# Attention output formed transposed, and the SSD half of the output projection done early

## What is computed

```
hn = rms_norm(x, norm_mix);  q, k, v, z, xbc, dt = split(hn @ w_in)
attn = rms_norm(softmax(q k^T / 8) v, attn_norm)            # 8 heads of 64, 2 kv heads; norm over 512
y = ssd_fwd + ssd_bwd + xs * d_skip                          # 8 heads of 64, chunks of 128
ssm = rms_norm(y * silu(z), ssm_norm)                        # in two groups of 256
x1 = x + concat(attn, ssm) @ w_out
h = rms_norm(x1, norm_ffn);  top 4 of h @ w_router + b_router, softmax weights
out = x1 + sum over the 4 experts of weight * ((min(g,7) sigmoid(1.702 g)) (clip(u,-7,7) + 1)) @ w_down + b_down
      with g = h @ w_gate + b_gate, u = h @ w_up + b_up
```

## Time and profile before

| | us |
|---|---|
| median of 3 runs | 1430.92 |
| runs | 1429.87 to 1432.21 |
| the profiled execution | 1428.61 |
| its span, first to last instruction | 1426.8 |
| PE busy | 1316.1 (92%) |
| DVE busy | 449.8 (32%) |
| ACT busy | 218.2 (15%) |
| POOL busy | 191.2 (13%) |

### The profile page before, as it was taken

The page is one execution under the profiler, slowest core; times in us unless marked ns, Lnnn a source line. Parts: engine busy times, 40 slices in busy tenths (PEclk is TensorE's granted clock), DMA queues, the critical chain, the costliest instruction groups (busy, mean ns, idle before and its releaser), DMA issues.

```text
span 1426.8 us, 40195 instructions
## 1 busy us (share of the span) xinstructions
PE 1316.1 (92%) x18053; PEld 811.1 (57%) x18053; DVE 449.8 (32%) x1049; ACT 218.2 (15%) x487; POOL 191.2 (13%) x142
## 2 busy tenths in 40 slices
PE   5999989998799999999998988998999998999973
PEld 3466676665456666666565554655655654666651
DVE  3653577545322222222221221322221321322310
ACT  2132244331101101100110010110010011001100
POOL 0000210000101221111121111121121122012111
PEclk9999999998799999999999999999999999999996
DMA  8000320006999999999999999999999999999992
GB/s 348 4 1 0 148 107 1 31 30 246 384 373 373 394 391 380 403 383 400 395 397 402 396 412 399 407 403 393 411 396 404 406 399 410 389 415 381 407 404 84
DMA packets 79359, 446.18 MB, mean 313 GB/s; under 512 B 13226, under 2 KB 21490, under 8 KB 30034
## 3 DMA queue, kind: packets, MB, share of 16 engines
q1 hardware_dynamic: 63922, 425.85, 74.1%
q0 software_dynamic: 15120, 17.20, 5.7%
q10 hardware_dynamic: 144, 0.52, 0.1%
HBM read 433.30 MB, written 14.94 MB: 314 GB/s over the span
## 4 chain that ended last, share of the span: by engine, by line
SPq 43%; PE 43%; DMA 7%; issue 2%; DVE 2%; POOL 1%; ACT 0%; DVEq 0%; POOLq 0%; ACTq 0%
SPq L609 43%; PE pair L1832 19%; PE pair L1580 7%; DMA ring<-in_w_down 4%; PE pair L1564 4%; PE pair L1541 2%; DMA rest<-in_w_gate 2%; PE pair L1732 2%; PE pair L1672 2%; PE pair L1694 1%; PE pair L1791 1%; POOL ring L711 1%; DMA rest<-normed_rows,rest 1%; DVE rest L1038 1%; PE pair L1767 1%
## 5 line engine op out<-in xcount | busy, mean ns | idle before, releaser
L1832 PE MATMUL pair<-ring,rest 128*32 128x256 f32 x14832 | 847.1, 383 | 44.6 <-DMA ring<-in_w_down 23.6
L1832 PEld LDWEIGHTS pair<-ring,rest 128*32 128x32 f32 x14832 | 479.3, 110 | 358.4 <-issue 29.1
L751 POOL DMA_INDIRECT out<-rest x82 | 128.3, 1565 | 776.8 <-ACT rest L995 722.2
L1038 DVE TENSOR_TENSOR rest<-pair,rest 128x512 f32<-128x512 f32 (+4 forms) x113 | 88.9, 787 | 440.0 <-PE pair L1832 424.5
L995 ACT ACTIVATE rest<-rest 128x256 f32<-128x256 f32 x82 | 36.5, 500 | 541.4 <-DVE rest L1038 541.4
L1580 PE MATMUL pair<-ring 128*128 128x512 f32 (+1 forms) x256 | 99.8, 548 | 1.4 <-DVE ring L1038 0.8
L1580 PEld LDWEIGHTS pair<-ring 128*128 128x128 f32 x256 | 48.9, 193 | 48.3 <-issue 44.7
L1038 DVE TENSOR_TENSOR rest<-rest 128x512 f32<-128x512 f32 (+7 forms) x98 | 62.8, 651 | 32.6 <-ACT rest L977 26.7
L977 ACT ACTIVATE rest<-rest 128x512 f32<-128x512 f32 (+3 forms) x34 | 24.4, 718 | 299.5 <-DVE rest L1367 299.5
L1832 PE MATMUL pair<-rest 128*32 128x256 f32 x912 | 56.2, 384 | 6.5 <-DMA rest<-in_w_down 4.3
L1334 DVE TENSOR_SCALAR rest<-pair 64x1 int32<-64x1 f32 (+3 forms) x34 | 5.2, 152 | 176.0 <-issue 172.4
(11 more groups left out here) (177 smaller groups left out, 873.6 us busy)
## 6 DMA issues: line engine op xcount, KB each, us to landing
ring<-in_w_up SPq DMA_DIRECT2D x121, 1024.0 KB, 28.4
ring<-in_w_gate SPq DMA_DIRECT2D x120, 1024.0 KB, 28.8
ring<-in_w_down SPq DMA_DIRECT2D x120, 1024.0 KB, 29.3
rest<-in_w_gate SPq DMA_DIRECT2D x8, 1024.0 KB, 29.2
rest<-in_w_down SPq DMA_DIRECT2D x8, 1024.0 KB, 29.0
rest<-in_w_up SPq DMA_DIRECT2D x7, 1024.0 KB, 27.8
ring<-in_w_in SPq DMA_DIRECT2D x1, 4160.0 KB, 15.3
ring<-in_x SPq DMA_DIRECT2D x8, 512.0 KB, 6.0
```

Source lines behind the costliest of these rows:

```text
L751: p.indirect_dma_start(out=out_rows, out_offset=bass.IndirectOffsetOnAxis(ap=sidx[vi.ring][:, g:g + 1].bitcast(I32), axis=0), in_=yrow_b[v ...
L1038: return v.tensor_tensor(out=out, in0=a, in1=b, op=op)
L1832: last = T.matmul(ps[q * TOK:(q + 1) * TOK, g * QW:(g + 1) * QW], x, pieces[slot][:, kk, q * QW:(q + 1) * QW], start=(k == 0 and g % 2 == ...
```

## The change

- **Product with v.** Before, the transposed probabilities (128 x 128) are PE's weights and v (128 x 64) moves; a head's output has tokens on partitions. Now v is the weights (64 columns) and the probabilities move; the two heads of a pair go to partitions 0 to 63 and 64 to 127 of bank 7, so the output is transposed as it is formed, and its transposes fall away.
- **Norm of the attention rows.** The inverse softmax sums are now needed along the free axis: DVE takes the reciprocal of the sums spread over 512 columns, PE transposes that (`rs`), ACT copies it, and one DVE product takes bank 7 to `mixaT`. ACT squares it, PE adds the squares over partitions (`an`, 8 records with one moving column), ACT makes the factor, and it is applied when the output projection is added to x1 (scalar_tensor_tensor). The gain attn_norm is multiplied into w_out's first half by POOL, once.
- **SSD half.** `combine`, the transposes (`ts`) and the SSD half of the output projection (`os`) run every second step from step 1, 3 and 5; OP, TH, LG come two steps earlier. The skip term and the gating by silu(z) move from DVE to POOL; the sigmoid of z comes before ACT's copy of `yd3`; DVE's backward carry of the states (`carry_back`) comes behind the maxima of pair 0.
- **For the last tile** `choose` comes at step 17, ahead of the product that empties bank 7, and `weigh` ahead of the last logits.
- **Buffers.** w_out is loaded in two halves into different places, and several small buffers move, so that pieces 2 to 14 are loaded during the mixer.

```
-RING_AT = (0, 1, 16, 4, 5, 14, 15, 6, 7, 8, 9, 12, 13, 2, 3, 10, 11)
+RING_AT = (0, 1, 12, 13, 16, 4, 5, 6, 7, 8, 2, 14, 15, 10, 11, 3, 9)
...
-TM, OP, TH, LG = 7, 8, 9, 10
+YO, TS, OS = 1, 3, 5
+RS, OP, TH, LG = 5, 6, 7, 8
...  SyncE
+            sp.dma_start(w_out_s, w_out_d[:, KT // 2:KT, :]).then_inc(s_wos, 16)
...
+            load(2, 0)
+            load(3, 0)
...
+            store(0)
+            store_normed(0)
+            sp.wait_ge(s_y0, NT)
+            load(4, 0)
+            sp.wait_ge(s_ys, NT)
+            wait_full(sp, f"yf{NT - 1}")
+            for n in (5, 6, 7):
+                load(n, 0)
+            store(1)
+            store_normed(1)
+            wait_full(sp, f"os{NT - 1}b")
+            for n in (8, 9):
+                load(n, STREAM[n][1])
+            sp.wait_ge(s_ost, 16 * 2)
+            load(10, STREAM[10][1])
+            store(2)
+            store_normed(2)
+            wait_full(sp, f"p{NPAIR - 1}b")
+            load(11, STREAM[11][1])
+            sp.wait_ge(s_of, NPAIR)
+            load(12, STREAM[12][1])
+            store(NT - 1)
+            for n in (13, 14):
+                load(n, STREAM[n][1])
 
             sp.wait_ge(s_ost, 16 * NT)
             sp.wait_ge(s_hst, 16 * NT)
             wait_full(sp, f"lg{NT - 1}")
-            for n in (13, 14, 15, 16):
+            for n in (15, 16):
...  POOL
+            for n in range(KT // 2):
+                nc.gpsimd.tensor_tensor(out=w_out_a[:, n, :], in0=w_out_a[:, n, :],
+                                        in1=pc_att[:, n:n + 1].to_broadcast([P, DM]), op=ALU.mult).then_inc(s_wog, 1)
+
+            pool.wait_ge(s_xdt, NT)
+            for c in range(NT):
+                nc.gpsimd.tensor_tensor(out=cut(xs[:, c, :], SH, HD), in0=cut(xs[:, c, :], SH, HD), in1=over(dsk, HD),
+                                        op=ALU.mult).then_inc(s_skip, 1)
+            for c in range(NT):
...
+                nc.gpsimd.tensor_tensor(out=ydsb[:, c, :], in0=ydsb[:, c, :], in1=xs[:, c, :], op=ALU.add).then_inc(s_y0, 1)
...
+                nc.gpsimd.tensor_tensor(out=zs[:, c, :], in0=zs[:, c, :], in1=xc[:, c, :], op=ALU.mult).then_inc(s_zg, 1)
...  DVE, in the loop over steps
+                if s == 0:
+                    carry_back()
+                if turn_at(s, RS - 1, 4) is not None:
...
+                    v.reciprocal(by_head(sqT), over(sums[:, i % 2, :], HD)).then_inc(s_rs, 1)
+                if s == LG + 4 * (NT - 2) + 1:
+                    for c in range(NT - 1):
+                        choose(c)
+                if turn_at(s, RS, 4) is not None:
+                    i = turn_at(s, RS, 4)
+                    wait_taken(dve, f"rs{i}")
                     dve.wait_ge(s_of, 4 * i + 4)
...
+                    tt(mixaT[i % 2], cut(bank[7][:, :], NH // 2, P), cut(rsT, NH // 2, P)).then_inc(s_ofree, 1)
+                if turn_at(s, TS, 2) is not None:
+                    i = turn_at(s, TS, 2)
                     dve.wait_ge(s_yn, i + 1)
...  PE
-                for h in range(2):
-                    head = 2 * j + h
-                    kv = head // (NH // NKV)
-                    for kt in range(NT):
-                        last = T.matmul(bank[7][:, head * HD:(head + 1) * HD], probsT[p % 2 * 2 + h][:, kt, :],
-                                        vs[:, kt, kv * HD:(kv + 1) * HD], start=(kt == 0), stop=(kt == NT - 1))
+                kv = 2 * j // (NH // NKV)
+                for kt in range(NT):
+                    for h in range(2):
+                        last = T.matmul(bank[7][h * HD:(h + 1) * HD, j * P:(j + 1) * P], vs[:, kt, kv * HD:(kv + 1) * HD],
+                                        probsT[p % 2 * 2 + h][:, kt, :], start=(kt == 0), stop=(kt == NT - 1))
```

More of the change, by code:

```diff
@@ L1278, in _ @@
+                if turn_at(s, OP, 4) is not None:
+                    t = turn_at(s, OP, 4)
                     if t == NT - 1:
-                        for c in range(t):
-                            choose(c)
-                        for c in range(t):
-                            weigh(c)
                         ps = wait_full(dve, "cue")
@@ L1725, in _ @@
+                if turn_at(s, OP, 4) is not None:
+                    t = turn_at(s, OP, 4)
+                    pe.wait_ge(s_ofree, t + 1)
+                    pe.wait_ge(s_wog, KT // 2)
+                    begin(f"an{t}")
+                    out_half(f"op{t}a", mixaT[t % 2], w_out_a, 0, {2: lambda: attn_squares(t)})
                     if t == NT - 1:
                         before_last_tile()
[L1727 to L1733 removed]
@@ L1734, in _, with first_rows @@
-                    end(last, f"op{t}b")
-                if turn_at(s, TH) is not None:
-                    t = turn_at(s, TH)
+                    def first_rows():
+                        wait_taken(pe, f"op{t}a")
+                        transposes(f"th{t}a", [x1[:, t, n * P:(n + 1) * P] for n in range(4)])
+                    out_half(f"op{t}b", mixaT[t % 2], w_out_a, 1, {3: first_rows})
+                if turn_at(s, TH, 4) is not None:
+                    t = turn_at(s, TH, 4)
                     wait_taken(pe, f"op{t}b")
```

269 lines of the change are left out of this document (153 added, 116 removed).

## The result

| | kernel before | changed kernel |
|---|---|---|
| median of the runs | 1430.47 us (4 runs, 1429.87 to 1432.21) | 1451.12 us (4 runs, 1448.53 to 1454.78) |
| profiled execution, its span | 1428.61, 1426.8 | 1454.78, 1452.5 |
| ratio | | **1.0152**, 95% interval 1.0134 to 1.0169 |

The change makes the kernel slower by 20.6 us.

What follows compares the result with a forecast made beforehand. PE was taken to bound the mixer, PE then DMA the experts. PE's work -9.8, waits +28.5 and the stretch behind -5.1 gave +13.6 on 1428.61, so 1442; median 2.3 above: 1444 us, range 1415 to 1458 (8 in 10).

Steps and rivals of the forecast that it cites:

- clock: PE in the mixer: three new waits of 4 us and more could cost 2 us each; not in the sum.
- waits: PE in the mixer: new waits for other engines sum to 35.8 us against 7.3 before, +28.5.
- PE's work: Mixer: v product saves 13.3 us, sums of squares add 3.5, together -9.8 us.
- Chunk 3: Start of the mixer: PE waits 7.7 us for decay tiles because Pool's products slow DVE's last six.
- Reciprocal: DVE in the mixer: the 512-wide reciprocal takes 2.8 us, bounds 0.7 and 3.4.
- GpSimd beside VectorE: Mixer: DVE SBUF products go one per Pool operation; full blocking by the skill's rule would add some 3.5 us of wait.
- Behind the mixer: Last addition to first expert matmul: 18.9 us instead of 24.0, so -5.1 us (0 to -8).
- Early pieces worth nothing: Experts: earlier weight loads gain nothing since the ring is full by 480 us; distance to the end unchanged, 1054 us.
- The rival's 11 us: Experts: four more pieces landed at the first matmul save 11 us, 1433, or 1407 with the faster rival (together 0.05).
- The waits don't come: Mixer: PE waits 7 to 12 us as before, so -15 to -10 us, 1418; chance 0.20.
- the waits halve: Mixer: PE waits 20 us instead of 35.8, so -2 us, 1429; chance 0.12.
- The change doesn't speed the product with v: Mixer: the two heads' columns don't overlap, PE's work +3.5 instead of -9.8, 1451; chance 0.06 shared with clock added.

Runs made afterwards that it cites:

- e1: Changed kernel with GpSimd's four gain products for w_out's attention half moved behind its skip additions and z gatings: 1447.4 us, ratio to the kernel before 1.0135.
- e3: Changed kernel with seven unused matmuls of constants on PE ahead of its wait for chunk 3's decay tiles: 1451.8 us, ratio to the kernel before 1.0162.
- e12: Changed kernel with unused matmuls of constants ahead of four PE waits in the middle of the mixer: 1448.6 us, ratio to the kernel before 1.0130.
- e11: Changed kernel with weight pieces 13 to 16 loaded only after the first gathered rows landed: 1450.7 us, ratio to the kernel before 1.0151.
- e5: Changed kernel with GpSimd's skip, addition and gating of chunks 1 to 3 and its gains held until VectorE carried the backward states: 1448.1 us.
- e9: Mended kernel with pieces 13 to 16 loaded only after the first gathered rows landed: 1426.3 us, ratio to the kernel before 0.9985.
- e4: Changed kernel with the loads of weight pieces 2 to 14 issued where the kernel before issued them: 1456.5 us, ratio to the kernel before 1.0181.
- mended kernel: Changed kernel with late GpSimd work, an 8-column reciprocal plus copy, and a new order in the steps: 1432.8 us, ratio to the kernel before 1.0024.

## Why the prediction held, and which steps of it did not

Sign, range and the main mechanism held: forecast 1444, measured 1451, and PE's new waits are the largest term. Against the profiled execution, which lies 12.6 us above the sum of 1442.2, four terms were off: clock +14.4, waits -8.5, PE's work +3.7, the stretch behind +3.9. That the median came within 7 us is in part luck: the two largest of these have opposite signs.

- *Clock (the step that failed).* It stood outside the sum, as up to 2 us for each of three long waits. Measured: 14.4 us more of rows at half rate in the profiled execution, since shorter waits did it as well: behind 1.73 us (237.82) the v product took 1.98 us, not 1.09. Nor does a wait of given length decide it: in e1 the last v product, behind 1.76 us, took 1.09, and in the changed kernel 1.98 (358.10). What it costs in time is less: nothing at the start (e3), about 4 us in the middle (e12), and 4.4 us in the last steps, which e11 with the same mixer didn't have. So a part of the 14.4 belongs to this one execution; how much the other three had isn't on record beyond their granted clocks.
- *Waits:* forecast 28.5 more, measured 20.0. Chunk 3 was right (7.7 and 6.4; matmul at 201.5 for 203.1). Pairs 0 to 5 with the reciprocal were put at 9.5 and waited 7.0; the SSD rows of step 5 at 4.1 and waited 2.1, those of step 9 at 5.9 and 3.6; steps 13 and 14 at 2.3 and 1.7, steps 16 to 18 at 4.3 and 2.6. Step 8, where none was forecast, had 1.8. PE at half clock asks later, so clock and waits can trade against each other: behind the last v product PE waited 0.85 us at half clock and 2.15 in e1 at the full one. Their sum was +34.4 where the forecast had +28.5.
- *PE's work:* forecast -9.8, measured -6.1. The v product at 1.0 us was right (1.02 from start to start), and so were the squares, 0.95 us a tile (0.81 from start to start). The old v product was not: 1.83 us is its cost ahead of scores, as in the earlier trace rows, and in most of the other steps it was 1.73, so some 12 us were saved and not 13.3. Not in the sum were the transposes of the sums (16 records, 2.4 us, for which only 1.6 of others went) and a step in front of the new product: eight transposes ahead of it take 1.02 us from start to start, and 0.93 ahead of the old one, 1.4 us for 16 pairs.

```profile
267.23 1.09 PE L1620 MATMUL pair<-rest,ring 128*128 128x128 f32 x8
268.25 1.09 PE L1750 MATMUL pair<-ring,rest 128*64 128x128 f32 x16
```

- *Reciprocal:* 3.34 us, near the bound of 3.4 and not at 2.8: 6.2 ns a column, where the forecast had 5.1. The eight repeats of the Trainium skill, "VectorE: DVE Perf Modes", "First, the fixed hardware budget", would be 8.3 ns by an estimate with that page's 0.96 GHz; the measurement lies between the two.
- *GpSimd beside VectorE:* one VectorE product for each GpSimd operation, as I took it from the earlier trace rows. What was missed is that VectorE's very small operations suffer too (e5). The full blocking of the Trainium skill, "SBUF — State Buffer", "Who interferes with whom", would add 0.69 us for each of the seven; the trace has 13.51 us for them, which is the time of GpSimd's own operations, so the rule doesn't hold here.
- *Behind the mixer:* forecast -5.1, measured -1.2. The index was ready 12.8 us behind the last addition (forecast 12.1). The gather's rows then took 7.9 us and not 4.5, since SyncE issued four pieces from 376.55 on, not two. e9 shows the term: without them it is at most 4.7.
- *Early pieces worth nothing:* held as far as this can be read: 1053.6 us to the end, and 1052.2 in e4 without them, where kernels with the same experts and the same early pieces have 1050.1 (e1) to 1054.7 (e12). The rival's 11 us are excluded, 2 us are not.
- *The rivals:* "The waits don't come" and "the waits halve" fell. "The change doesn't speed the product with v" fell at 224.54, where 16 records took 1.09 us. The drain at a switch of tiling, of the Trainium skill, "TensorEngine Tiling (Array Packing)", "Key Properties", can be no more here than the 0.09 us by which the transposes ahead of the product are longer; the row behind it starts 1.02 us after it. Whether these 0.09 us are the drain no run separates.

## What to carry to other kernels

Where PE is the bound with 5% of slack, work taken from it is worth nothing unless the chain of the other engines is shorter than PE's new step: here 6 us saved on PE came with 20 us of waits, and mending one showed the next. Before moving work to GpSimd, list what VectorE does in that time, the tiny operations too. And what stands behind the last store on the path (index, store, gather) should have the DMA queues to itself: four loads issued 15 us later gave 6 us in the mended kernel, and nothing to be measured in the changed one, where the index was late.

## What the runs showed of the hardware

- A VectorE operation on 128x2 values takes 0.17 us alone and up to 1.33 (e1) beside a GpSimd product of SBUF operands; row maxima that read PSUM stay at 1.29.
- VectorE's reciprocal: 0.20 us for 8 columns, 3.34 for 512 (6.2 ns a column), whereas a copy that spreads 8 columns over 512 takes 0.43.
- Matmuls that compute nothing hold the granted clock through a wait (0.99 for 0.64 over 16 us).
- The same instructions behind the same wait can run at either clock: behind 0.85 and 0.86 us, a row of four records took 3.78 us in the changed kernel and 1.98 in e11.
